# Key sums of half the heads in two single passes each, the sub-layer factor behind the transposes, and rows transposed sooner

## The reference, cut to what matters

```
u = rms_norm(h, g_mix) @ w_in                       # q, k, v of both mixers
ya = diff_attention(qa, ka, va, lam, g_subln, ...)  # 4 heads of width 128
o  = rms_norm(o, g_subln) * (1.0 - lam_init)        # its last line, per head
yb = stick_breaking_attention(qs, ks, vs)           # 8 heads of width 64:
     log_1mb = where(strict, log_sigmoid(-z), 0)
     between = cumsum(log_1mb, reverse) - log_1mb   # sums over later keys
     a = exp(where(strict, log_beta + between, -inf))
h = h + concat(ya, yb) @ w_out
h = h + cross_attention(...)                        # keys and values: mem @ w_xkv
```

## Time and profile before

| | |
|---|---|
| time before, median of 3 runs | 907.1 us (906.73 to 908.7) |
| profiled execution: its own time | 909.25 us |
| its span, first to last instruction | 907.5 us |
| mean granted TensorE clock | 0.996 |
| busy: PE, POOL, DVE, ACT | 877.2, 687.4, 468.5, 423.4 us |
| the stage of the change (strips 8 and 9 with the heads) | about 123 to 163 us |

### The profile page before, as it was taken

The page is one execution under the profiler, slowest core; times in us unless marked ns, Lnnn a source line. Parts: engine busy times, 40 slices in busy tenths (PEclk is TensorE's granted clock), DMA queues, the critical chain, the costliest instruction groups (busy, mean ns, idle before and its releaser), DMA issues.

```text
span 907.5 us, 13290 instructions
## 1 busy us (share of the span) xinstructions
PE 877.2 (97%) x5378; PEld 758.6 (84%) x5378; DVE 468.5 (52%) x671; ACT 423.4 (47%) x574; POOL 687.4 (76%) x395
## 2 busy tenths in 40 slices
PE   7999999999999999999999899999999999999998
PEld 5798876897799999998888688777678899999996
DVE  3578644244336322334788799857974432223333
ACT  4773347463263433333673456246345463444430
POOL 3799357778459999999898677840608979999882
PEclk9999999999999999999999999999999999999999
DMA  8785344346135566654754524530205446665531
GB/s 305 273 274 195 117 139 139 119 139 228 67 122 186 189 213 200 207 204 151 267 189 140 201 85 162 174 129 1 94 1 184 148 145 206 203 213 201 188 136 47
DMA packets 65795, 149.29 MB, mean 165 GB/s; under 512 B 4912, under 2 KB 10192, under 8 KB 65616
## 3 DMA queue, kind: packets, MB, share of 16 engines
q1 hardware_dynamic: 65744, 148.59, 49.0%
HBM read 147.53 MB, written 1.05 MB: 164 GB/s over the span
## 4 chain that ended last, share of the span: by engine, by line
PE 72%; DVE 13%; POOL 5%; ACT 3%; DMA 3%; issue 2%; SPq 0%; DVEq 0%; ACTq 0%
PE ps L1667 62%; POOL w_lo L643 5%; PE ps L1842 3%; PE ps L1816 2%; DMA raw<-in_w_in 2%; PE ps L1828 1%; PE ps L1754 1%; DVE xn L1387 1%; DVE arena L1394 1%; DVE arena L1184 1%; DVE arena L1389 1%; ACT w_hi L683 1%; DMA arena<-in_xT 1%; DVE arena L1054 1%; DVE xn L1556 1%
## 5 line engine op out<-in xcount | busy, mean ns | idle before, releaser
L643 POOL TENSOR_TENSOR w_lo<-raw,w_hi 128x512 fp32r<-128x512 f32 (+2 forms) x370 | 675.6, 1865 | 165.4 <-ACT w_hi L683 157.8
L683 ACT ACTIVATE w_hi<-raw 128x1024 fp32r<-128x1024 f32 (+1 forms) x192 | 247.0, 1327 | 268.3 <-PE ps L1667 137.7
L1667 PE MATMUL ps<-w_hi,x_hi 128*128 128x512 f32 (+1 forms) x672 | 267.1, 397 | 2.6 <-POOL w_lo L643 1.5
L1667 PE MATMUL ps<-w_hi,x_lo 128*128 128x512 f32 (+1 forms) x672 | 261.0, 388 | 0.0
L1667 PE MATMUL ps<-w_lo,x_hi 128*128 128x512 f32 (+1 forms) x672 | 260.7, 388 | 0.0
L1667 PE MATMUL ps<-x_hi,w_hi 128*128 128x256 f32 x704 | 201.0, 286 | 0.6 <-DVE arena L1035 0.6
L1667 PE MATMUL ps<-x_hi,w_lo 128*128 128x256 f32 x704 | 199.2, 283 | 0.0
L1667 PE MATMUL ps<-x_lo,w_hi 128*128 128x256 f32 x704 | 199.2, 283 | 0.0
L1667 PEld LDWEIGHTS ps<-w_hi,x_hi 128*128 128x128 f32 x672 | 126.7, 188 | 35.0 <-issue 7.6
L1667 PEld LDWEIGHTS ps<-w_hi,x_lo 128*128 128x128 f32 x672 | 126.5, 188 | 26.4
L1667 PEld LDWEIGHTS ps<-w_lo,x_hi 128*128 128x128 f32 x672 | 126.9, 189 | 23.3
(11 more groups left out here) (258 smaller groups left out, 788.0 us busy)
## 6 DMA issues: line engine op xcount, KB each, us to landing
raw<-in_w_in SPq DMA_DIRECT2D x35, 1024.0 KB, 5.3
raw<-in_w_up SPq DMA_DIRECT2D x32, 1024.0 KB, 5.4
raw<-in_w_down SPq DMA_DIRECT2D x32, 1024.0 KB, 4.8
raw<-in_w_xkv SPq DMA_DIRECT2D x8, 1024.0 KB, 5.1
raw<-in_w_out SPq DMA_DIRECT2D x8, 1024.0 KB, 4.9
raw<-in_w_xq SPq DMA_DIRECT2D x4, 1024.0 KB, 5.1
raw<-in_w_xo SPq DMA_DIRECT2D x4, 1024.0 KB, 4.9
raw<-in_w_o_a SPq DMA_DIRECT2D x3, 1024.0 KB, 4.8
```

The lines of the kernel that those rows point to most:

```text
L643: x = nc.gpsimd.tensor_tensor(LO[s % 2][:, 2048 * q + d0:2048 * q + d1], RAW[n % 3][:, d0:d1], HI[s % 2][:, 2048 * q + d0:2048 * q + d1].b ...
L683: nc.scalar.activation(HI[s % 2][:, 2048 * q + c0:2048 * q + c1], RAW[n % 3][:, c0:c1], ACT.Copy).then_inc(hi_done, 1)
L1667: last = T.matmul(dst, l, r, start=start and i == 0, stop=stop and i == 2, skip_group_check=w_stationary)
```

## The change

Five things. (1) `z_sums` of groups 0 and 1 no longer multiplies the float32 softplus; ACT copies it to float32r in `x_hi` (L813 of the changed kernel), DVE subtracts the rest to `x_lo` (L1278), and PE runs the sums on each part, with the triangle and the ones as a float32r copy, `tri2`, made by DVE. Groups 2 and 3 stay as they were. (2) The factor `gsub` is no longer a row multiplied in `sub_norm`: it is loaded as one value per partition and applied behind the transposes, as the scale of ACT's copy and in DVE's subtraction. (3) The squares and sums of `sub_norm` go ahead of the `z_sp` steps. (4) The transposes of block 0 go ahead of strip 9, and those of block 1 behind its eighth step. (5) ACT's copies of weights move: the second half of strip 9 to the front of the stage, the first half of strip 10 behind the first two Exps, the second half of strip 10 behind the last two.

```diff
@@ -100,6 +100,7 @@
...
+        tri2 = XH[0][:, 1792:2048]
...
-        gsub = small(128)
+        gsub = small(1)
...
-            misc.append((gsub, a["g_subln"][0].partition_broadcast(P)))
+            misc.append((gsub, a["g_subln"][0].rearrange("(p o) -> p o", o=1)))
...
@@ -780,10 +783,13 @@
                 act.wait_ge(z_pv, 2 * half + 2)
                 nc.scalar.activation(sb_cols(XH, half), bank(2), ACT.Copy).then_inc(sb_hi, 1)
 
+            def ya_to_hi(t):
+
+                act.wait_ge(ya_done, t + 1)
+                nc.scalar.activation(ya_cols(XH, t), ya_tile, ACT.Copy, scale=gsub).then_inc(ya_hi, 1)
+
+            hi(9)
             for half in range(2):
-                if half == 0:
-                    hi(9, 0)
-
                 js = (2 * half, 2 * half + 1)
                 if half == 1:
                     sb_to_hi(0)
@@ -792,6 +798,8 @@
                     if j >= 2:
                         act.wait_ge(z_cum, j - 1)
                     link(nc.scalar.activation(wide(sbz[j % 2]), z_bank(j), ACT.Abs))
+                if half == 1:
+                    ya_to_hi(0)
                 for j in js:
                     link(nc.scalar.activation(sbz[j % 2], sbz[j % 2], ACT.Exp, scale=-1.0))
                 for j in js:
@@ -799,20 +807,24 @@
                 if half == 0:
                     act.wait_ge(sub_sq, 1)
                     link(nc.scalar.activation(y0_s, ss_s, ACT.Ln, scale=1.0 / P, bias=eps))
+                if half == 0:
+                    for j in js:
+                        act.wait_ge(z_sp, j + 1)
+                        nc.scalar.activation(XH[0][:, 768 * j:768 * j + 768], sbz[j], ACT.Copy).then_inc(z_hi, 1)
                     nc.scalar.activation(y0_s, y0_s, ACT.Exp, scale=-0.5).then_inc(sub_y0, 1)
-                    hi(9, 1)
-                if half == 1:
-                    for t in range(NT):
-                        act.wait_ge(ya_done, t + 1)
-                        nc.scalar.activation(ya_cols(XH, t), ya_tile, ACT.Copy).then_inc(ya_hi, 1)
-                for j in (2 * half, 2 * half + 1):
+                else:
+                    ya_to_hi(1)
...
-                if half == 1:
+                if half == 0:
+                    hi(10, 0)
+                else:
+                    hi(10, 1)
                     sb_to_hi(1)
-                hi(10 + half)
+                    hi(11)
...
             unit_loop(0, U_X, post_diff, hook_diff, early_diff)
+            V.tensor_copy(tri2, cst[:, C_TRI:C_TRI + 256]).then_inc(tri_ready, 1)
+            ya = xn[:, :, 0:512]
+            link(V.tensor_tensor(sq1.rearrange("p (t c) -> p t c", t=NT), ya, ya, ALU.mult))
+            V.tensor_reduce(ss_s, sq1.rearrange("p (s c) -> p s c", c=P), AX.X, ALU.add).then_inc(sub_sq, 1)
+
             def sub_norm():
 
-                ya = xn[:, :, 0:512]
-                link(V.tensor_tensor(sq1.rearrange("p (t c) -> p t c", t=NT), ya, ya, ALU.mult))
-                V.tensor_reduce(ss_s, sq1.rearrange("p (s c) -> p s c", c=P), AX.X, ALU.add).then_inc(sub_sq, 1)
                 dve.wait_ge(sub_y0, 1)
                 newton(rs_s, ss_s, y0_s, P)
                 yv = ya.rearrange("p t (h c) -> p t h c", c=P)
                 rv = rs_s.rearrange("p (t h) -> p t h", t=NT)
-                link(V.tensor_tensor(yv, yv, bc(rv.unsqueeze(3), [P, NT, 4, P]), ALU.mult))
-                link(V.tensor_tensor(yv, yv, bc(gsub.unsqueeze(1).unsqueeze(1), [P, NT, 4, P]), ALU.mult))
-
+                V.tensor_tensor(yv, yv, bc(rv.unsqueeze(3), [P, NT, 4, P]), ALU.mult).then_inc(ya_ready, 1)
+
+            def ya_to_lo(t):
+
+                dve.wait_ge(ya_hi, t + 1)
+                V.scalar_tensor_tensor(ya_cols(XL, t), ya_tile, gsub, ya_cols(XH, t).bitcast(f32),
+                                       ALU.mult, ALU.subtract).then_inc(ya_lo, 1)
 
             def sb_to_lo(half):
 
@@ -1248,18 +1266,19 @@
             for half in range(2):
                 if half == 1:
                     sb_to_lo(0)
+                    ya_to_lo(0)
                 for j in (2 * half, 2 * half + 1):
                     dve.wait_ge(z_ln, j + 1)
                     V.scalar_tensor_tensor(wide(sbz[j % 2]), z_bank(j), 0.0, wide(sbz[j % 2]),
                                            ALU.max, ALU.add).then_inc(z_sp, 1)
                 if half == 0:
+                    for j in range(2):
+                        dve.wait_ge(z_hi, j + 1)
+                        c = slice(768 * j, 768 * j + 768)
+                        V.tensor_tensor(XL[0][:, c], sbz[j], XH[0][:, c].bitcast(f32), ALU.subtract).then_inc(z_lo, 1)
                     sub_norm()
-                    signal(ya_ready, 1)
                 else:
-                    for t in range(NT):
-                        dve.wait_ge(ya_hi, t + 1)
-                        V.tensor_tensor(ya_cols(XL, t), ya_tile, ya_cols(XH, t).bitcast(f32),
-                                        ALU.subtract).then_inc(ya_lo, 1)
+                    ya_to_lo(1)
                 evac(8 + half, vm[:, :, 512 * half:512 * half + 512], rows=rstd_n[:, 2:4])
             sb_to_lo(1)
             residual(11, gbuf[0])
...
             def z_sums(j):
 
-                pe.wait_ge(z_sp, j + 1)
-                b, sp = z_bank(j), sbz[j % 2]
-                for hh in range(2):
-                    T.matmul(b[:, hh, :], tri, sp[:, 384 * hh:384 * hh + 384], start=False, stop=True,
-                             skip_group_check=True)
-                    last = T.matmul(b[:, hh, P:S], negones, sp[:, 384 * hh + S:384 * hh + 384],
-                                    start=False, stop=True, skip_group_check=True)
+                b = z_bank(j)
+                if j < 2:
+                    pe.wait_ge(tri_ready, 1)
+                    c = 768 * j
+                    parts = [(z_hi, XH[0][:, c:c + 768], tri2[:, 0:P], tri2[:, P:2 * P]),
+                             (z_lo, XL[0][:, c:c + 768], tri2[:, 0:P], tri2[:, P:2 * P])]
+                else:
+                    parts = [(z_sp, sbz[j % 2], tri, negones)]
+                for ready, sp, within, after in parts:
+                    pe.wait_ge(ready, j + 1)
+                    for hh in range(2):
+                        T.matmul(b[:, hh, :], within, sp[:, 384 * hh:384 * hh + 384], start=False, stop=True,
+                                 skip_group_check=True)
+                        last = T.matmul(b[:, hh, P:S], after, sp[:, 384 * hh + S:384 * hh + 384],
+                                        start=False, stop=True, skip_group_check=True)
                 last.then_inc(z_cum, 1)
 
...
@@ -1975,8 +2002,8 @@
                 else:
                     pe.wait_ge(ya_ready, 1)
                     for t in range(NT):
-                        strip(9, 4 * t, 4 * t + 4)
                         if t == 1:
+                            strip(9, 0, 8)
                             pe.wait_ge(ya_lo, 1)
                         for q in range(4):
                             last = T.transpose(ya_tile[:, q, :], xn[:, t, P * q:P * q + P], ident)
```

7 lines of the change are left out of this document (5 added, 2 removed).

## The result

The changed kernel took **913.17 us** in the median of 6 executions (904.66 to 915.38), the kernel before 906.91 (905.58 to 908.70, 6 executions beside them): the ratio over these executions is 1.0049, 95% interval 1.0028 to 1.007. One of the six, at 904.66, is where the forecast was; the other five lie 4.8 to 8.5 us above the kernel before. The profiled execution is one of the five: 914.71 us, span 912.8.

A forecast was written before the change was run, and what follows sets the result against it. PE, busy 97% of the span, was taken as the bound. Savings of 1.5 and 1.95 us less a new wait of 1.4 gave 2.05 us, so 905.1 us against a median of 907.1; range 903.3 to 907.6.

The forecast's parts named there:

- Key sums, 1.5 us: Key sums of groups 0 and 1 on PE: 16 float32r products take 1.9 us instead of 3.47, saving 1.5.
- Transposes, 1.95 us: PE's wait ahead of block 1's transposes goes, because block 0's subtraction is done in time: 1.95 us saved.
- the 1.8 us to spare: `z_sp` of groups 2 and 3 ends near 150, PE reaches those sums near 151.8: covered by 1.8 us.
- The new wait at strip 11, 1.4 us: At strip 11's third step PE waits 1.4 us for POOL, which has twelve pieces to do after ACT's late copy.
- the collision put at nothing: DVE and POOL collisions would make strip 11's wait 2.2 us; none expected, since DVE reads PSUM there.
- slower, by POOL's backlog: Rival: late work on strips 10 to 12 runs into strip 13; with 4.5 us of lateness 909.6 us; chance 0.06.

The follow-up runs named there:

- e4: e1 with the key sums of groups 0 and 1 in float32 again, without the copies and subtractions feeding them: 906.06 us, 0.9970 of the kernel before.
- e1: The changed kernel with both halves of strip 10 copied by ACT where the kernel before does it: 904.96 us, 0.9959 of the kernel before.
- g4: e1 with PE's old order: four steps of strip 9 before the first block of transposes, four between the blocks: 904.49 us, 0.9953 of the kernel before.
- g3: The changed kernel, with POOL beginning strip 12 only when ACT has copied all of it: 905.57 us, 0.9974 of the kernel before.

## Why the prediction was wrong

**Key sums, 1.5 us: right in kind, mis-sized.** In the changed kernel the sixteen products stand between 133.83 and 136.57, 2.74 less two strip products, 2.28 against 3.47: 1.2 us, and e4 against e1 says 1.1. PE there:

```profile
134.28 0.39 PE L1977 MATMUL ps<-x_hi 128*128 128x384 f32 x1
134.51 0.22 PE L1979 MATMUL ps<-x_hi 128*128 128x128 f32 x1
134.57 0.39 PE L1977 MATMUL ps<-x_lo,x_hi 128*128 128x384 f32 x1
```

The short product took 0.06, near the 0.07 that I had. The long one behind it took 0.23, as much as 512 columns take, and I had 0.17 from its columns. The very first, which stands behind a product of the strip, did take 0.17 (134.05 to 134.22). `z_hi` and `z_lo` made no wait.

**Transposes, 1.95 us: right.** The shift grows from -0.96 to -3.04, 2.08 us. But g4 shows that the order on PE, to which I gave the gain, was not needed for it, and that the steps behind had more than the 1.8 us to spare that I gave them.

**The new wait at strip 11, 1.4 us: right.** The shift falls by 1.24, and the row is:

```profile
173.57 0.50 PE L1686 MATMUL ps<-w_hi,x_hi 128*128 128x512 f32 x1 [1.15 <-POOL w_lo L646]
```

With the terms as measured, 1.2 + 2.1 - 1.2, the change would have won 2.1 us; PE came to the key sums 0.2 us late (133.83 against 133.63), so at strip 11 it was 1.8 us ahead, where my sum has 2.05. g3, which is the changed kernel without the lock-out, has 0.9974, 2.4 us under the kernel before, and the one execution of the changed kernel that escaped took 904.66, 2.3 us under. By place g3's PE is 1.6 us ahead at 507 us (505.36 against 506.98); the interval of its ratio, 1.3 to 3.5 us, holds that as well as 2.05. So without the lock-out the sum would have stood, with a gain a few tenths smaller at strip 11, and it comes that near partly by luck, because its errors cancel: it had the saving on the key sums 0.3 us too high and left out the 0.2 of coming late to them, but had the transposes 0.1 too low and the wait 0.2 too long.

**The step that failed** is the collision put at nothing, in the sentences behind that wait: "With collisions between DVE and POOL ... it is 2.2; none is expected, since DVE reads PSUM there. Behind it POOL's backlog (strip 12, eight more pieces) ends about 0.5 us ahead of the copy of strip 13, so it goes no further." I followed the backlog on POOL and on PE and looked for DVE only where it feeds the key sums. In strip 11 DVE adds the residual from PSUM and then multiplies `h` by `gain`, both in SBUF, and the backlog now stood over that. The trace of before had the answer in kind: three such products of 1.43 to 1.68 us in place of 0.69, under a run of sixteen pieces. I had not asked for DVE's rows there. In the run, the product was held for 7.94 us in place of 0.69, and PE waited 6.04 us for it.

**The rival "slower, by POOL's backlog"** named the backlog, but on another path (strips 13 and 14, and not DVE's product of strip 11), and not the price. It let a collision cost one piece, about 1 us, so that four would have to come together, and got 0.06. One collision cost 6.3 us of PE and the 2.2 of the clock behind it. The price could not be read from the trace of before, where the collisions end behind one piece; that they might not was a bound that I left out.

**The range** ended at 907.6 for the same reason: its upper end added small waits, and had no case in which a wait grows with the length of a queue.

## What to carry to other kernels

When a piece of work is moved behind a wait, lay the backlog that it makes over every engine that shares something with the late one, not only over the engine that consumes its result: here the consumer waited 1.2 us, where 1.4 was computed, and a bystander 7.2. A product with two SBUF inputs on DVE beside a long unbroken run of short instructions on POOL is such a place. A pause in the run (a wait for something that is due anyway) took 7 us off in g3 at no cost that shows, and reading one input from PSUM does the same where the program allows it. And where a kernel's times fall into two heaps, find out which heap the profile shows before its rows are added up.
